# Expert matrices in 8 KB runs per partition, and a gather that reads every fourth channel

## What is computed

```python
def grouped_moe(x, w_router, b_router, w1, w3, w2):      # 256 tokens, 32 experts, 2 chosen per token
    ...
    def expert_block(args):
        tok, e = args
        xb = x_pad[tok]                                   # the tokens of expert e, 2048 channels
        hb = jax.nn.silu(xb @ w1[e]) * (xb @ w3[e])       # w1, w3: 2048 x 512 per expert
        return hb @ w2[e]                                 # w2: 512 x 2048 per expert
```

## Time and profile before

| | us |
|---|---|
| median of three runs (lowest, highest) | 1466.75 (1466.39, 1469.31) |
| span of the profiled execution, first to last instruction | 1466.0 |
| TensorE matmul busy in it | 1296.9 (88%) |
| TensorE weight load busy | 721.7 (49%) |
| VectorE, ScalarE, GpSimd busy | 455.2, 353.1, 243.0 |
| DMA moved | 473.81 MB, mean 323 GB/s |

### The profile page before, as it was taken

The page is one execution under the profiler, slowest core; times in us unless marked ns, Lnnn a source line. Parts: engine busy times, 40 slices in busy tenths (PEclk is TensorE's granted clock), DMA queues, the critical chain, the costliest instruction groups (busy, mean ns, idle before and its releaser), DMA issues.

```text
span 1466.0 us, 17030 instructions
## 1 busy us (share of the span) xinstructions
PE 1296.9 (88%) x6870; PEld 721.7 (49%) x6870; DVE 455.2 (31%) x648; ACT 353.1 (24%) x530; POOL 243.0 (17%) x62
## 2 busy tenths in 40 slices
PE   3897989999989999998989898989989898998983
PEld 3887989978743433333433333333433333343331
DVE  5545995642352130311303031121303022130306
ACT  4332322443321121211212121121212121121211
POOL 3767586565100000000000000000000000000001
PEclk9998999999989999999999999999999999999997
DMA  7554535547789999999999999999999999999991
GB/s 275 165 173 144 173 127 189 173 172 251 253 311 387 387 387 387 387 387 387 387 387 387 387 387 387 387 387 387 387 387 387 387 387 387 387 387 387 387 387 76
DMA packets 237572, 473.81 MB, mean 323 GB/s; under 512 B 9594, under 2 KB 10170, under 8 KB 236642
## 3 DMA queue, kind: packets, MB, share of 16 engines
q1 hardware_dynamic: 234256, 471.90, 88.5%
q10 hardware_dynamic: 3282, 1.43, 0.5%
HBM read 471.20 MB, written 2.10 MB: 323 GB/s over the span
## 4 chain that ended last, share of the span: by engine, by line
PE 64%; DMA 13%; DVE 11%; SPq 5%; ACT 4%; issue 2%; POOL 1%; ACTq 0%; DVEq 0%
PE psum L629 16%; PE psum L603 15%; PE psum L643 8%; PE psum L576 8%; PE psum L452 8%; DMA ring<-in_w_dram 7%; PE psum L472 7%; DMA area_g<-in_w_dram 6%; SPq L308 5%; DVE area_g L988 4%; ACT area_c L842 2%; POOL w_low L392 1%; DVE area_a L1252 1%; DVE area_a L1066 1%; DVE area_a L1253 1%
## 5 line engine op out<-in xcount | busy, mean ns | idle before, releaser
L603 PE MATMUL psum<-ring,area_c 128*64 128x512 f32 x1536 | 340.4, 595 | 25.8 <-DMA ring<-in_w_dram 25.8
L392 POOL TENSOR_TENSOR w_low<-ring,w_high 128x2048 fp32r<-128x2048 f32 (+1 forms) x42 | 225.2, 5371 | 112.8 <-ACT w_high L707 112.8
L603 PEld LDWEIGHTS psum<-ring,area_c 128*64 128x64 f32 x1536 | 106.5, 137 | 240.2 <-issue 191.3
L842 ACT ACTIVATE area_c<-psum,ln_chan 128x128 f32<-128x128 f32 x264 | 99.2, 456 | 402.9 <-PE psum L576 402.9
L452 PE MATMUL psum<-in_high,w_high 128*128 128x256 f32 x576 | 168.2, 292 | 25.2 <-POOL w_low L392 9.3
L398 POOL TENSOR_TENSOR area_b<-area_b,area_c 128x1024 f32<-128x1024 f32 x1 | 3.2, 3234 | 1079.1 <-ACT area_b L878 1079.1
L629 PE MATMUL psum<-ring,area_d 128*64 128x512 f32 x768 | 173.3, 596 | 0.4
L452 PE MATMUL psum<-in_low,w_high 128*128 128x256 f32 x576 | 166.8, 290 | 0.0
L452 PE MATMUL psum<-in_high,w_low 128*128 128x256 f32 x576 | 166.7, 289 | 0.0
L643 PE MATMUL psum<-area_d,one_hot_gt 128*128 128x512 f32 x256 | 126.5, 617 | 34.7 <-DVE area_a L1253 23.5
L707 ACT ACTIVATE w_high<-ring 128x2048 fp32r<-128x2048 f32 x56 | 107.0, 1914 | 186.3 <-PE psum L452 114.2
(11 more groups left out here) (178 smaller groups left out, 1055.0 us busy)
## 6 DMA issues: line engine op xcount, KB each, us to landing
ring<-in_w_dram SPq DMA_DIRECT2D x288, 1024.0 KB, 14.4
slot<-in_w_dram SPq DMA_DIRECT2D x48, 1024.0 KB, 14.3
area_g<-in_w_dram SPq DMA_DIRECT2D x48, 1024.0 KB, 14.1
ring<-in_w_in_dram SPq DMA_DIRECT2D x40, 1024.0 KB, 5.1
ring<-in_w_out_dram SPq DMA_DIRECT2D x16, 1024.0 KB, 5.0
area_a<-in_x_dram SPq DMA_DIRECT2D x2, 1024.0 KB, 7.8
out_dram<-area_b SPq DMA_DIRECT2D x4, 512.0 KB, 2.6
area_g<-in_ln_in_g_dram SPq DMA_DIRECT2D x1, 1024.0 KB, 14.9
```

The costliest lines, as they stand in the source:

```text
L392: nc.gpsimd.tensor_tensor(low[:, tiles], raw_unit(u)[:, tiles], high[:, tiles].bitcast(F32), ALU.subtract).then_inc(pool_low, 1)
L603: mm = pe.matmul(psum[i * CAP:(i + 1) * CAP, j // UNITS, :], gathered[:, kk, i * CAP:(i + 1) * CAP], w[:, i, k, :], start=kk == 0, stop=kk ...
L842: ins = act.activation(gathered[:, k, :], psum[:, 2 + g % 2, k % 4 * P:(k % 4 + 1) * P], ACT.Identity, scale=ln_chan[:, 2, k:k + 1], bias= ...
```

## The change

The loads of w1 and w3 read the matrix so that partition p gets the four consecutive rows 4 p to 4 p + 3 of a quarter, one contiguous run of 8 KB. Block k of a quarter then holds channels 4 p + k, so the gather takes, for its block j, every fourth of the 512 channels as stationary operand, and the drain takes gain and shift from a new tile `gain` in the same channel order, which two small DMAs on SyncE's queue fill. The loads of w2 stay as they are. The number of matmuls, weight loads and drains, their shapes and their order stay as they are.

```diff
+        gain = sb("gain", [P, 2, KT])
...
             sp.wait_ge(units_done, UNITS * (N_IN + 1))
+            for r, src in enumerate((ln1_g[0], ln1_b[0])):
+                sp.dma_start(gain[:, r, :].rearrange("p (q k) -> p q k", q=UNITS),
+                             src.rearrange("(q p k) -> p q k", q=UNITS, p=P)).then_inc(s_gain, 16)
             sp.dma_start(area_g[:, 0, :], spread(ln1_g[0])).then_inc(s_g, 16)
...
                     if j < 8:
-                        src = (w1, w3)[j // 4][0, e].rearrange("(q k p) f -> q p k f", q=4, p=P)[j % 4]
+                        src = (w1, w3)[j // 4][0, e].rearrange("(q p k) f -> q p k f", q=4, p=P)[j % 4]
...
             def gather(it, g):
 
                 for j in range(4):
-                    k = 4 * g + j
                     for t in range(TT):
                         mm = pe.matmul(psum[:, 2 + g % 2, j * P:(j + 1) * P],
-                                       area_b[:, t, k * P:(k + 1) * P],
+                                       area_b[:, t, g * CW:(g + 1) * CW].rearrange("p (s k) -> p k s", k=UNIT)[:, j, :],
                                        one_hot[:, t].rearrange("p i s -> p (i s)"),
                                        start=t == 0, stop=t == TT - 1)
...
                         ins = act.activation(gathered[:, k, :], psum[:, 2 + g % 2, k % 4 * P:(k % 4 + 1) * P],
-                                             ACT.Identity, scale=ln_chan[:, 2, k:k + 1], bias=ln_chan[:, 3, k:k + 1])
+                                             ACT.Identity, scale=gain[:, 0, k:k + 1], bias=gain[:, 1, k:k + 1])
...
+            act.wait_ge(s_gain, 16 * 2)
             keep_gathered(0, (0, 1))
```

More of the change, by code:

```diff
@@ L211, in hybrid_layer @@
         gathered = area_c[:].rearrange("p k s -> p (k s)")[:, 0:KT * P].rearrange("p (k s) -> p k s", k=KT)
-        s_rt, s_g2 = sem("router_weights_loaded"), sem("ln2_rows_loaded")
+        s_rt, s_g2, s_gain = sem("router_weights_loaded"), sem("ln2_rows_loaded"), sem("gain_loaded")
         s_x = [sem(f"x_loaded{t}") for t in range(TT)]
```

## The result

| us | before | changed |
|---|---|---|
| median (lowest, highest), four runs each | 1467.33 (1466.39, 1469.31) | 1557.72 (1555.42, 1559.56) |
| profiled execution: device time, span | span 1466.0 | 1556.66, 1554.8 |

The ratio is 1.061, with a 95% interval of 1.0595 to 1.0625: slower, as forecast, but by 90 us where the forecast had 68, and 7 us beyond the end of its range.

The account below looks back on a forecast made before the run. It took the loop as DMA-bound at 65.06 us per step, TensorE close behind at 61.65. Without DMA's limit 1425.8 us, plus 16 x 6.7 for stepped weight loads and 2.2 ahead of the loop: 1535 us, range 1426 to 1551.

Parts of the forecast that it names:

- what bounds the loop: Expert loop: TensorE's own pace of 61.65 us per step on prefetched slots, then DMA's 65.06 us once they are used up.
- what the loads are worth: Loop's DMA: if it no longer limits, 37.9 us over fifteen periods and 3.0 us of last-step waits vanish, together 40.9.
- weight loads already set the gather's pace: Gather: 111.6 ns from load to load, as in logit matmuls with four times less moving data, so nothing covers slower loads.
- the gain DMAs cost nothing: Two gain DMAs on SyncE's queue ahead of the first gather: hidden, since that gather drains only after 415 us.
- I take +110 ns: Gather's stepped weight loads: price per load chosen between 87, 118 and 125 ns; 61 exposed loads give 6.7 us per step.
- DVE's absolute time per stepped float: Price for the gather's weight loads from DVE reductions: 128 columns at 1.85 ns, 237 ns per load, +125.
- The price by DVE's ratio: Price for the gather's weight loads from DVE's stepped-to-consecutive ratio: 111.6 x 1.78 = 199 ns per load, +87.
- TensorE's moving operand: Price for the gather's weight loads if a stepped float costs four neighbours, 1.80 ns: 230 ns per load, +118.
- Rival 4: Loop: clock at its lower level for one 3.6 us unit per step after the slower gather; 1593 us, chance 0.05.
- The two gathers ahead of the loop: Before the loop: 32 stepped weight loads, about 20 counted at full clock, adding 2.2 us (0 to 4).
- first rival: Gather and loop loads: stepped weight loads are free and the DMA loads faster; 1429 us, chance 0.25.
- the second: Gather: half price, the stepped load partly covered at +25 to +80 ns; 1450 to 1504 us, chance 0.10.

Follow-up runs that it names:

- the step of two: Against the kernel before: loads in 4 KB runs, gather reading every second channel of 256, gain tile to match; 1432.53 us, ratio 0.9755.
- the step of three: Against the kernel before: 8 KB loads, gather reading every third channel, values wrong but same work; 1491.35 us, ratio 1.0159.

## Why the prediction was right and wrong

**Right:** what bounds the loop (two paces, 61.65 and 65.06 us), what the loads are worth (40.9 us; 42 measured), that packets of 8 KB are moved whole (140324 packets for "about 140,000"), that the DMA waits vanish and the gain is lost behind TensorE, that weight loads already set the gather's pace, and that the gain DMAs cost nothing (the first gather starts no later). The sign and the mechanism hold. Below 42 ns per load the change would have been a gain; the step of two, at 6 ns, is one, and the step of three, at 63 ns, is a loss of 24 us.

**Wrong:** the size, which left the range by 7 us. The profiled spans are 88.8 us apart where the sum had 68.4, and two terms make up the 20 us between them.

| term | predicted | measured |
|---|---|---|
| growth per step | 6.7 us (61 loads x 110 ns) | 7.65 us, so 14 us more in fifteen steps |
| clock | none in the forecast | 6.2 us in fifteen steps |
| calls ahead of the loop | +2.2 us | +4.4 us, less 1.0 by an earlier start |
| last step | +3.7 us | +2.4 us |

1. *"I take +110 ns"* is the step that failed, and the larger part of the error. Of the three prices, the highest, DVE's absolute time per stepped float (1.85 ns, 237 ns per load, +125), gives 7.6 us per step, and 7.65 were measured. The price by DVE's ratio (+87) was the wrong reading: the loads at four different steps follow a time per 16-byte piece, not a factor on the engine's own pace. Taking a middle between readings that the table above separates cost 14 us. Part of the fit is luck. The double call's loads grew by 122 ns and nearly all of the 64 are exposed, which comes to the same as 61 loads at 125. And no run shows why TensorE's moving operand (1.80 ns for four neighbours) or DVE should have the price of a weight load; that the figures agree is all that is known.
2. *Rival 4, "The clock falls as well"*, was priced as a case of its own, 5% and 58 us, with none of it in the forecast or in the upper end. This is nearly all of the 7 us by which the time left the range: the range's end of 1551 already held +125 ns, and without the dips' 6.2 us the time would be about 1551.5. The clock fell together with the forecast and at a tenth of that price, a dip of 1.4 to 1.7 us in four of fifteen steps. The rows it rested on the earlier trace rows pointed at the right thing, a thin stretch on TensorE followed by a pause.
3. *"The two gathers ahead of the loop"*: there are three calls before the first expert unit, 48 loads, as the first unit of a step stands behind the call with g = 2. In the last step, counted from its first unit, that call is then missing. The number of calls was right (16 x 4 + 2 = 66), so the miscount moves loads from one term to the other, and the two terms together are 5.8 us where the sum had 5.9.

One reference in the prediction is wrong: a price of nil leads to its first rival (1429), not to the second. That rival's case was measured with the new loads alone, at 1426.7; it is under 1429 because DMA needs 61.3 us for a step and not the 62.6 that 410 GB/s gave.

## What to carry to other kernels

A layout change that makes DMA runs long moves the step to whoever reads the data next; ask which instruction reads it how often, and put the permutation where it is read once (here ScalarE's four passes, 2 us) and not where it is read in every step. Before giving an operand a step, look for what covers the load: the same slower weight load was worth 2.7 us under 512-column matmuls and over 120 us under 128-column ones. And when several rows price an unknown, decide whether they measure a time or a ratio before averaging them.

## What the runs showed of the hardware

- A float32 weight load of 128 columns has a pace of 112 ns or 1.84 ns per 16-byte piece of SBUF that it touches, whichever is longer (118, 175, 234, 240 ns at steps 2, 3, 4, 8). With a piece for every float, three engines pay nearly the same on top: weight loads 122 / 128 = 0.95 ns per float, ScalarE's pass of 1024 floats 0.94 (about 1.19 us to 2.14), DVE's pass of 1024 floats 0.92 (1.23 us to 2.17).
- In a full queue, HBM to SBUF in 2 KB runs came at 387 GB/s and in 8 KB runs at 422 to 426; a mix of two thirds 8 KB at 409.
- In the loop the granted clock fell to its lower level for some 4 us after a stretch in which matmuls were busy all the time by the profile, but paced by weight loads at 234 ns and more, followed by transposes and a pause. With the whole call at 175 ns per load or less it never fell; with half a call of consecutive loads and two pauses it fell once.
